# A two-layer hybrid decoder trunk in fp32 on one core: when the attention output of layer 0 is scaled by its norm and turned

## The chip, the cores and the metric

The kernel runs on one core of one Trainium2 chip. The metric is the device time of one execution in microseconds (us). Before the change the median of three runs is 2280.72 us (2280.49 to 2282.51).

## The reference, cut to what matters

The program runs a trunk of two layers over 1024 tokens of width 1024. Each layer norms its input, projects it, mixes it (layer 0: differential attention beside a causal pooling mixer), projects the mixer's output with `w_out`, adds it to the residual stream, and adds a SwiGLU FFN. The change lies between the attention of layer 0 and its output projection:

```python
# layer 0; 4 heads ("units"), values of width 128
def block(i):                                   # 128 queries
    s = einsum('bqmhd,bkmhd->bmhqk', qb, k) * scale - slopes * dist     # two maps m
    p = softmax(where(dist >= 0, s, -inf))
    a = p[:, 0] - lam * p[:, 1]
    return einsum('bhqk,bkhd->bqhd', a, v)
ya = diff_attention(q, k, v, lam, slopes)
ya = rmsnorm(ya, ev_subln_gain) * (1.0 - lambda_init)   # per head and token, over 128 values
yb = multiscale_pool(u, pool_w, pool_scale)
x = x + concatenate([ya, yb], -1) @ ev_w_out            # 1024 x 1024
x = x + swiglu_ffn(x, ...)
```

## The kernel before, in words

Every fp32 product is made of three products: each factor is split into a rounded high part and a low part (value minus high part), and high·high, high·low and low·high are summed (`mm3`). ScalarE (ACT) writes most high parts, VectorE (DVE) and GpSimd (POOL) the low parts. The five engines run programs of their own that are written out by hand in one fixed order each; semaphores with counts order them against each other. Nothing is scheduled by a planner.

**The attention of layer 0** runs over 32 tiles n = 8u + i: unit (head) u = 0 to 3, query block i = 0 to 7, with 128(i+1) keys. A tile passes through these steps: PE makes the scores of both maps (`score`, L971 and L972; two tiles ahead), DVE adds the bias and takes the maximum (`biased`, L2030), ACT takes the exponent (`expo`, L1505), DVE combines both maps (`combine`, L2052; counts `c_ok`), PE transposes the result into PSUM (`turn`, L991; waits for `c_ok`), ACT copies it to SBUF (`turned`, writes PT), PE multiplies it with the values (`weigh`, L1007), and ACT squares the result and writes it, divided by the softmax denominator, to Y (`scaled`: L1536, then the copy Y; counts `o_ok`). From tile 9 on, PE also computes one block of the output projection of the pooling half beside each tile (`out_block`, 12 products of 128x256, 32 blocks in all), which DVE adds to X (`add_block`, L2059). Blocks 0 to 22 run beside the attention, 23 to 31 behind it.

**Norm and turn of Y.** GpSimd makes 1/rms of a unit from its sums of squares (`unit_power(u)`, L859 and L861, counts `y_rs`). Behind the last tile and three `add_block`s DVE multiplies Y by it, one instruction for each of the 8 token blocks over all four units (L2163, counts `y_ok`). Then PE transposes Y, unit by unit (`turn_y(j)`, L1171, 8 transpositions, all four wait for the 8 instructions); ACT writes the high part HH of a turned unit with the sub-norm's gain (`y_hi`, copy HH), DVE the low part HL (`y_lo`, L2133). Two units fit in PSUM banks 0 to 3, which the scores use before, so `turn_y(2)` and `turn_y(3)` wait for `y_lo(0)` and `y_lo(1)`. The turns stand between the blocks 27, 28, 30 and 31.

**Output projection of the attention half.** For two token blocks PE first makes the products with the weight group `WOh`, `WOl` (units 0 and 1, `out_part(2, ...)`), then those with `WO3h`, `WO3l` (units 2 and 3, `out_part(3, ...)`), 24 products of 128x512 each; the next six token blocks take both together. It waits once, for all four `y_lo`. GpSimd writes the low parts of these groups: `WO3l` (`low_w("g3", ...)`) before `unit_power(3)`, `WOl` (`low_w("g2", ...)`) behind it, each as soon as ACT's high part is there. The norm of the FFN follows.

## Time and profile before

| | |
|---|---|
| runs (median; lowest to highest) | 2280.72 us; 2280.49 to 2282.51 |
| the profiled execution: its own time, and its span | 2289.15 us, 2287.4 us |
| granted TensorE clock, mean | 0.983 of full speed |
| busy: PE / DVE / ACT / POOL | 2204.0 / 1268.6 / 884.5 / 795.8 us |
| attention of layer 0, and the stretch behind it up to the FFN | from about 227 us to 440 us of the span |

The span goes from the first to the last instruction; 1.75 us of the execution's own time lie around it. PE (TensorE, products) is busy for 96% of the span; its loads of weights (PEld) lie beside. In the rows of a timeline the columns are the start in us of the span, the duration, the engine, the line, the operation, the output and its inputs, and how many such instructions follow in a row; a bracket gives the idle time of the engine just before and what ended it. The ends of PE instructions are modelled and overlap the next start, so for PE the distance from start to start is what counts.

### The profile page before, as it was taken

To read this page: it belongs to the slowest core of one execution; us is meant where nothing else is said; L and a number is where in the kernel's file an instruction comes from. 1 tells how busy PE (TensorE), PEld (TensorE's weight loads), DVE (VectorE), ACT (ScalarE), POOL (GpSimd) and SP (SyncE) were. 2 spreads that over 40 slices of the span, in tenths; PEclk is the share of its full clock that TensorE was granted. 3 is DMA by queue.
4 is the path that set the end of the run, shared out by engine and by line. 5 is a ranking of instruction groups with operands and counts; after the bars stand their busy time and mean duration, and the time that the engine had idled before them with its cause. 6 is when DMAs were issued, how large, how long until landed. Compare 5 with 4: busy or idle time off the path is not lost.

```text
span 2287.4 us, 30362 instructions
## 1 busy us (share of the span) xinstructions
PE 2204.0 (96%) x10600; PEld 1840.3 (80%) x10600; DVE 1268.6 (55%) x1771; ACT 884.5 (39%) x1443; POOL 795.8 (35%) x538
## 2 busy tenths in 40 slices
PE   7999897999999999999999998999999999999999
PEld 6876787888888887888888877887888888887887
DVE  4244775676656554558322336566775555554555
ACT  4123874443333333435211126662443333333433
POOL 0022542266666772002000131220367766762000
PEclk9999899999999999999999998999999999999999
DMA  5021120035555547674111111102045555547665
GB/s 178 10 78 28 38 84 19 19 121 192 194 193 167 165 159 272 192 239 137 37 44 48 46 55 38 38 19 74 19 147 194 193 196 164 166 154 267 193 192 194
DMA packets 219222, 283.87 MB, mean 124 GB/s; under 512 B 11504, under 2 KB 120560, under 8 KB 219120
## 3 DMA queue, kind: packets, MB, share of 16 engines
q1 hardware_dynamic: 218832, 282.50, 38.3%
q8 instruction: 58, 0.95, 0.2%
q14 instruction: 44, 0.36, 0.1%
q10 hardware_dynamic: 288, 0.05, 0.0%
HBM read 199.67 MB, written 73.40 MB: 119 GB/s over the span
## 4 chain that ended last, share of the span: by engine, by line
PE 71%; issue 21%; DVE 4%; ACT 2%; POOL 2%; DMA 0%; POOLq 0%; DVEq 0%; SPq 0%; ACTq 0%
PE PS L1284 12%; PE PS L1285 12%; PE PS L1286 12%; PE PS L1311 6%; PE PS L1313 6%; PE PS L1312 6%; PE PS L1007 3%; PE PS L919 3%; PE PS L921 3%; PE PS L920 3%; PE PS L991 2%; POOL QRS L832 1%; PE PS L971 1%; PE PS L972 1%; PE PS L937 1%
## 5 line engine op out<-in xcount | busy, mean ns | idle before, releaser
L1799 DVE TENSOR_TENSOR LINEl<-LINE,HIGH 128x1024 fp32r<-128x1024 f32 x154 | 193.8, 1264 | 170.2 <-ACT HIGH L1342 169.9
L1342 ACT ACTIVATE HIGH<-LINE 128x1024 fp32r<-128x1024 f32 x154 | 162.5, 1059 | 236.6 <-PE PS L1313 232.2
L1311 PE MATMUL PS<-HIGH 128*128 128x512 f32 x616 | 241.8, 393 | 7.0 <-DVE LINEl L1799 7.0
L1312 PE MATMUL PS<-LINEl,HIGH 128*128 128x512 f32 x616 | 240.8, 391 | 0.0
L1313 PE MATMUL PS<-HIGH,LINEl 128*128 128x512 f32 x616 | 240.8, 391 | 0.0
L1799 DVE TENSOR_TENSOR SLOTl<-BLOCKS,RING 128x512 fp32r<-128x512 f32 x168 | 157.7, 939 | 96.8 <-ACT RING L1342 92.0
L807 POOL TENSOR_TENSOR ST<-ST 128x512 f32<-128x512 f32 x132 | 191.9, 1454 | 34.4 <-DMA ST<-in_ffn_w_down 25.7
L1342 ACT ACTIVATE RING<-BLOCKS 128x512 fp32r<-128x512 f32 x168 | 105.9, 631 | 227.7 <-PE PS L1286 223.6
L832 POOL TENSOR_TENSOR QRS<-QMS,EXPO 128x8 f32<-128x8 f32 x32 | 52.0, 1639 | 383.3 <-DVE QMS L1962 383.2
L1799 DVE TENSOR_TENSOR SLOTl<-SLOT,RING 128x512 fp32r<-128x512 f32 x126 | 134.4, 1066 | 86.6 <-ACT RING L1342 86.3
L1311 PEld LDWEIGHTS PS<-HIGH 128*128 128x128 f32 x616 | 116.3, 189 | 32.0 <-DVE LINEl L1799 8.3
L1313 PEld LDWEIGHTS PS<-HIGH,LINEl 128*128 128x128 f32 x616 | 116.3, 189 | 24.6
L1312 PEld LDWEIGHTS PS<-LINEl,HIGH 128*128 128x128 f32 x616 | 116.5, 189 | 24.2
L1007 PE MATMUL PS<-V,PT 128*128 (+1 forms) x864 | 118.2, 284 | 13.4 <-ACT Y L1342 11.6
L1007 PEld LDWEIGHTS PS<-V,PT 128*128 128x128 f32 x864 | 111.0, 200 | 24.5 <-ACT PT L1342 14.1
L1284 PE MATMUL PS<-B1h,RING 128*128 128x512 f32 x336 | 130.7, 389 | 0.0
L1285 PE MATMUL PS<-B1l,RING 128*128 128x512 f32 x336 | 130.7, 389 | 0.0
L1286 PE MATMUL PS<-B1h,SLOTl 128*128 128x512 f32 x336 | 130.7, 389 | 0.0
L1342 ACT ACTIVATE RING<-SLOT 128x512 fp32r<-128x512 f32 x126 | 79.2, 630 | 125.3 <-PE PS L1286 114.9
L779 POOL TENSOR_TENSOR SLOT<-BLOCKS 128x512 f32<-128x512 f32 x42 | 55.2, 1314 | 190.3 <-DMA BLOCKS<-in_ffn_w_up 190.3
L2030 DVE CUSTOM_DVE_ANT_0 PR<-PS,BIAS 128x128 f32<-128x128 f32 (+7 forms) x130 | 96.9, 748 | 31.1 <-PE PS L991 16.5
L812 POOL TENSOR_TENSOR RST<-MSQ,EXPO 128x1 f32<-128x1 f32 x32 | 22.9, 718 | 260.9 <-DVE MSQ L1816 260.9
(299 smaller groups left out, 5711.7 us busy)
## 6 DMA issues: line engine op xcount, KB each, us to landing
LINE<-hidden SPq DMA_DIRECT2D x154, 256.0 KB, 2.7
hidden<-HID SPq DMA_DIRECT2D x44, 512.0 KB, 4.4
ST<-in_ffn_w_down SPq DMA_DIRECT2D x44, 512.0 KB, 4.2
sums<-ST SPq DMA_DIRECT2D x22, 1024.0 KB, 6.1
hidden<-ST SPq DMA_DIRECT2D x22, 1024.0 KB, 6.7
LINE<-sums SPq DMA_DIRECT2D x88, 256.0 KB, 3.0
BLOCKS<-in_ffn_w_gate SPq DMA_DIRECT2D x42, 512.0 KB, 4.0
BLOCKS<-in_ffn_w_up SPq DMA_DIRECT2D x42, 512.0 KB, 5.2
```

The source lines that it names most:

```text
L807: nc.gpsimd.tensor_tensor(dst, x, y, op).then_inc(st_sum, 1)
L832: nc.gpsimd.tensor_tensor(QRS[:, 8 * b:8 * b + 8], QMS[:, 8 * b:8 * b + 8], EXPO[:, 0:8], ALU.pow).then_inc(qk_rs, 1)
L1007: last = pe.matmul(weighed(L, m, i), PT[m if L else i % 2][:, P * j:P * j + P], V[:, j, bass.ds(off, w)], start=(j == 0), stop=(j == i))
L1284: pe.matmul(dst, lh, rh[:, k, :], start=k == 0 and not adds_on, stop=False, skip_group_check=adds_on)
L1285: pe.matmul(dst, lh, rl[:, k, :], start=False, stop=False, skip_group_check=adds_on)
L1286: last = pe.matmul(dst, ll, rh[:, k, :], start=False, stop=k == 3, skip_group_check=adds_on)
L1311: pe.matmul(dst, hi[:, 0, ts], hi[:, 1, :], start=j == 0 and not adds_on, stop=False, skip_group_check=adds_on)
L1312: pe.matmul(dst, hi[:, 0, ts], lo[:, 1, :], start=False, stop=False, skip_group_check=adds_on)
L1313: pe.matmul(dst, lo[:, 0, ts], hi[:, 1, :], start=False, stop=j == NJ - 1, skip_group_check=adds_on).then_inc(dn_pe, 1)
L1342: return nc.scalar.activation(dst, src, ACT.Copy, **kw)
L1799: return v.tensor_tensor(dst, src, hi.bitcast(F32), ALU.subtract)
L2030: v.tensor_tensor_reduce(out=PR[m][t % 2][:, 0:keys], in0=PS[:, 1024 * m:1024 * m + keys], in1=table, scale=-1.0, scalar=3.0e38, op0=ALU.a ...
```

## The change

It moves the scaling and the turning of Y forward, and holds two low parts on GpSimd back:

- DVE scales Y by unit instead of by token block: `unit_scaled(u)` is one multiplication of 128 x 8 x 128 values. Units 0, 1 and 2 are scaled inside the attention, behind `combine` of tiles 14, 22 and 29; unit 3 behind blocks 23 to 25. `y_ok` now counts units.
- PE turns unit 0 before `turn` of tile 31, unit 1 before the last `weigh`, unit 2 behind block 25 and unit 3 behind block 28. The first two wait until DVE has read the last scores.
- ACT writes the high parts of units 0 and 1 before and behind the copy and scaling of tile 30's values; DVE writes their low parts ahead of `add_block(23)`.
- The products with `WOh`, `WOl` wait for the low parts of units 0 and 1 only, those with `WO3h`, `WO3l` for all four.
- GpSimd waits for `combine` of tile 31 (`c_ok`, 32) before `WO3l`, and for all four scalings (`y_ok`, 4) before `WOl`.

```diff
 # GpSimd
                     low_w("q3", QWl[3], QWs[3], QWh[3])
+                    pool.wait_ge(c_ok, TILES0)
                     low_w("g3", WO3l, WO3s, WO3h)
                     unit_power(3)
+                    pool.wait_ge(y_ok, UNITS)
                     low_w("g2", WOl, WO2s, WOh)
 # TensorE
+                def turn_y(j):
+                    if L == 0:
+                        pe.wait_ge(y_ok, j + 1)
+                        if j < 2:
+                            for m in range(2):
+                                pe.wait_ge(s_mx[m][0], 1 + TILES0)
...
+                            if g + i == TILES0 - 1:
+                                turn_y(0)
                             turn(0, 0, g, 0, i)
                             if g + i >= FILL_FROM:
                                 out_block(g + i - FILL_FROM)
+                    turn_y(1)
                     weigh(0, 0, UNITS - 1, NT * (UNITS - 1), 0, NT - 1)
...
-                    for blocks in ((23, 24, 25, 26, 27), (28,), (29, 30), (31,)):
-                        for k in blocks:
-                            out_block(k)
-                        turn_y((27, 28, 30, 31).index(blocks[-1]))
+                    for k in range(BLOCKS_IN, 4 * NT):
+                        out_block(k)
+                        if k in (25, 28):
+                            turn_y((25, 28).index(k) + 2)
...
-                pe.wait_ge(yt_lo, 4 * L + 4)
+                pe.wait_ge(yt_lo, 4 * L + (2, 4)[L])
                 pe.wait_ge(wo_lo, WO_AT[L] + (6, 3)[L])
...
+                pe.wait_ge(yt_lo, 4 * L + 4)
                 pe.wait_ge(wo_lo, WO_AT[L] + (6, 4)[L])
 # ScalarE
+                    score_done()
+                    y_hi(0)
                     turned(0, NT * (UNITS - 1), NT - 1)
-                    for n in (TILES0 - 2, TILES0 - 1):
-                        scaled(n)
+                    scaled(TILES0 - 2)
+                    y_hi(1)
+                    scaled(TILES0 - 1)
                     high_w("g2", WOh, WO2s)
 # VectorE
+                def unit_scaled(u):
+                    dve.wait_ge(y_rs, u + 1)
+                    dve.wait_ge(o_ok[0][0], 2 + NT * (u + 1))
+                    ys = Y[:, :, P * u:P * u + P]
+                    by = YRS[:, NT * u:NT * u + NT].rearrange("p (t o) -> p t o", o=1).broadcast_to([P, NT, P])
+                    v.tensor_tensor(ys, ys, by, ALU.mult).then_inc(y_ok, 1)
...
                         combine(i)
+                        if n in (14, 22, 29):
+                            unit_scaled(u - 1)
...
+                    y_lo(0)
+                    y_lo(1)
                     for k in range(23, 26):
                         add_block(k)
-                    dve.wait_ge(y_rs, UNITS)
-                    dve.wait_ge(o_ok[0][0], 2 + 8 * UNITS)
-                    for t in range(NT):
-                        ys = Y[:, t, :].rearrange("p (h d) -> p h d", d=P)
-                        by = YRS[:].rearrange("p (h t) -> p h t", t=NT)[:, :, t:t + 1].broadcast_to([P, 4, P])
-                        v.tensor_tensor(ys, ys, by, ALU.mult).then_inc(y_ok, 1)
-                    for j, blocks in enumerate(((26, 27), (28,), (29, 30), (31,))):
-                        for k in blocks:
-                            add_block(k)
-                        y_lo(j)
+                    unit_scaled(UNITS - 1)
+                    y_lo(2)
+                    for k in range(26, 29):
+                        add_block(k)
+                    y_lo(3)
+                    for k in range(29, 32):
+                        add_block(k)
```

What it moves on each engine, as the built programs have it. PE at tile 31, before: the last products of tile 30 with the values (V, PT), the transposition of the combined map (PR), block 22 (QWh, QWl with UH, UL), the products of tile 31, block 23.

```order
L1007 MATMUL PS<-V,PT_286 128x128 [waits o_okA0,t_eaA0]
L1007 MATMUL PS<-V,PT_286 128x128 x6
L991 MATMUL PS<-IDN,PR_291 128x128 [waits c_ok,t_eaA0]
L991 MATMUL PS<-IDN,PR_291 128x128 x7
L919 MATMUL PS<-QWh_81,UH_63 128x256 [waits od_add0]
L920 MATMUL PS<-QWl_77,UH_63 128x256
...
L1007 MATMUL PS<-V,PT_287 128x128 [waits o_okA0,t_eaA0]
L1007 MATMUL PS<-V,PT_287 128x128 x7
L919 MATMUL PS<-QWh_81,UH_63 128x256 [waits od_add0]
```

PE at the same place now (Y is the scaled attention output, IDN the identity):

```order
L1010 MATMUL PS<-V,PT_286 128x128 [waits o_okA0,t_eaA0]
L1010 MATMUL PS<-V,PT_286 128x128 x6
L1129 MATMUL PS<-IDN,Y 128x128 [waits s_mxB0,s_mxA0,y_ok]
L1129 MATMUL PS<-IDN,Y 128x128 x7
L994 MATMUL PS<-IDN,PR_291 128x128 [waits c_ok,t_eaA0]
L994 MATMUL PS<-IDN,PR_291 128x128 x7
L922 MATMUL PS<-QWh_81,UH_63 128x256 [waits od_add0]
L923 MATMUL PS<-QWl_77,UH_63 128x256
...
L1129 MATMUL PS<-IDN,Y 128x128 [waits s_mxB0,s_mxA0,y_ok]
L1129 MATMUL PS<-IDN,Y 128x128 x7
L1010 MATMUL PS<-V,PT_287 128x128 [waits o_okA0,t_eaA0]
L1010 MATMUL PS<-V,PT_287 128x128 x7
```

Two groups of 8 transpositions of Y have come in, one in front of tile 31's transposition and one in front of its products with the values; they wait for `y_ok` and for the maxima of both maps (`s_mx`).

DVE from `combine` of tile 31 on, before (PR: the maps; X with PS: a block added; HL: a low part of turned Y):

```order
L2052 SCALAR_TENSOR_TENSOR PR_291<-PR_291,SCB,PR_289 128x1024 [waits att_seq0]
L2059 TENSOR_TENSOR X<-PS,X 128x256 [waits od_pe0]
L2059 TENSOR_TENSOR X<-PS,X 128x256 [waits od_pe0,att_seq0]
L2059 TENSOR_TENSOR X<-PS,X 128x256 [waits od_pe0] x2
L2163 TENSOR_TENSOR Y<-Y,YRS 128x512 [waits o_okA0,y_rs]
L2163 TENSOR_TENSOR Y<-Y,YRS 128x512 x7
L2059 TENSOR_TENSOR X<-PS,X 128x256 [waits od_pe0] x2
L2133 SCALAR_TENSOR_TENSOR HL<-PS,COLS,HH 128x1024 [waits yt_hi]
L2059 TENSOR_TENSOR X<-PS,X 128x256 [waits od_pe0]
L2133 SCALAR_TENSOR_TENSOR HL<-PS,COLS,HH 128x1024 [waits yt_hi]
```

and now:

```order
L2073 SCALAR_TENSOR_TENSOR PR_291<-PR_291,SCB,PR_289 128x1024 [waits att_seq0]
L2080 TENSOR_TENSOR X<-PS,X 128x256 [waits od_pe0]
L2092 SCALAR_TENSOR_TENSOR HL<-PS,COLS,HH 128x1024 [waits s_mxA0,s_mxB0,yt_hi,att_seq0]
L2092 SCALAR_TENSOR_TENSOR HL<-PS,COLS,HH 128x1024 [waits s_mxB0,s_mxA0,yt_hi]
L2080 TENSOR_TENSOR X<-PS,X 128x256 [waits od_pe0] x3
L2103 TENSOR_TENSOR Y<-Y,YRS 128x8x128 [waits o_okA0,y_rs]
L2092 SCALAR_TENSOR_TENSOR HL<-PS,COLS,HH 128x1024 [waits o_peA0,yt_hi]
L2080 TENSOR_TENSOR X<-PS,X 128x256 [waits od_pe0] x3
L2092 SCALAR_TENSOR_TENSOR HL<-PS,COLS,HH 128x1024 [waits o_peA0,yt_hi]
L2080 TENSOR_TENSOR X<-PS,X 128x256 [waits od_pe0] x3
```

The 8 multiplications of 128x512 are gone from here; one of 128x8x128 is left, and two low parts of Y stand ahead of blocks 23 to 25. Three more such multiplications stand further up, each behind a `combine`.

GpSimd from the low part of the pooling half's last weight group (QWl) on, before:

```order
L853 TENSOR_TENSOR QWl_78<-QWs_74,QWh_82 128x1024 [waits wo_hi,y_rs]
L853 TENSOR_TENSOR WO3l<-WO3s,WO3h 128x2048 [waits wo_hi,wo_lo]
L859 TENSOR_TENSOR YSS<-YSS,EPSP 128x8 [waits y_sq,wo_lo]
L861 TENSOR_TENSOR YRS<-YSS,EXPO 128x8 [waits y_ms]
L853 TENSOR_TENSOR WOl<-WO2s,WOh 128x2048 [waits wo_hi,y_rs]
```

and now:

```order
L853 TENSOR_TENSOR QWl_78<-QWs_74,QWh_82 128x1024 [waits wo_hi,y_rs]
L853 TENSOR_TENSOR WO3l<-WO3s,WO3h 128x2048 [waits wo_hi,c_ok,wo_lo]
L859 TENSOR_TENSOR YSS<-YSS,EPSP 128x8 [waits y_sq,wo_lo]
L861 TENSOR_TENSOR YRS<-YSS,EXPO 128x8 [waits y_ms]
L853 TENSOR_TENSOR WOl<-WO2s,WOh 128x2048 [waits wo_hi,y_ok,y_rs]
```

The rows are the same five; two of them have one more semaphore to wait for, `c_ok` and `y_ok`.

## Rows read from the trace of the kernel before

**Rows 1.** The page's chain that ended last, by engine.

```profile
PE 71%; issue 21%; DVE 4%; ACT 2%; POOL 2%; DMA 0%; POOLq 0%; DVEq 0%; SPq 0%; ACTq 0%
```

**Rows 2.** Timeline of PE, 361 to 410 us.

```profile
361.34 1.80 PE L1007 MATMUL PS<-V,PT 128*128 128x128 f32 x14 [1.55 <-ACT Y L1342]
365.66 1.06 PE L991 MATMUL PS<-IDN,PR 128*128 128x128 f32 x8 [2.52 <-DVE PR L2052]
366.48 0.36 PE L919 MATMUL PS<-QWh,UH 128*128 128x256 f32 x1
...
368.54 2.02 PE L1007 MATMUL PS<-V,PT 128*128 128x128 f32 x16 [0.38 <-ACT Y L1342]
370.32 0.36 PE L919 MATMUL PS<-QWh,UH 128*128 128x256 f32 x1
...
377.24 0.28 PE L919 MATMUL PS<-QWh,UH 128*128 128x256 f32 x1
...
382.69 1.97 PE L1171 MATMUL PS<-IDN,Y 128*128 128x128 f32 x8 [4.93 <-DVE Y L2163]
...
388.25 0.36 PE L919 MATMUL PS<-QWh,UH 128*128 128x256 f32 x1
...
391.20 1.04 PE L1171 MATMUL PS<-IDN,Y 128*128 128x128 f32 x8
391.99 0.36 PE L919 MATMUL PS<-QWh,UH 128*128 128x256 f32 x1
...
393.50 1.04 PE L1171 MATMUL PS<-IDN,Y 128*128 128x128 f32 x8
397.06 0.50 PE L919 MATMUL PS<-WOh,HH 128*128 128x512 f32 x1 [2.52 <-DVE HL L2133]
...
404.26 0.39 PE L919 MATMUL PS<-WO3h,HH 128*128 128x512 f32 x1
...
409.70 0.39 PE L919 MATMUL PS<-WOh,HH 128*128 128x512 f32 x1
```

**Rows 3.** Stretches: from:to, length, busy of each engine, granted clock, DMA.

```profile
356.00:370.00 14.00, 9.55 (x78) 8.92 (x79) 7.81 (x7) 6.83 (x13) 4.51 (x1) 1.00 0.00 1
382.00:388.00 6.00, 5.31 (x25) 5.31 (x26) 3.01 (x6) 1.11 (x1) 0.00 (x0) 0.51 0.01 3
398.30:401.50 3.20, 3.20 (x9) 2.42 (x9) 0.00 (x0) 0.00 (x0) 0.00 (x0) 0.50 0.00 0
```

**Rows 4.** Timeline of DVE, tiles 22, 23, 30 and 31, and the tail.

```profile
321.86 1.14 DVE L2052 SCALAR_TENSOR_TENSOR PR<-PR,SCB,PR 128x896 f32<-128x896 f32 x1
...
325.62 0.42 DVE L2059 TENSOR_TENSOR X<-PS,X 128x256 f32<-128x256 f32 x1 [0.80 <-PE PS L921]
...
354.45 1.23 DVE L2030 CUSTOM_DVE_ANT_0 PR<-PS,BIAS 128x1024 f32<-128x1024 f32 x1 [0.82 <-PE PS L991]
...
360.17 5.34 DVE L2052 SCALAR_TENSOR_TENSOR PR<-PR,SCB,PR 128x1024 f32<-128x1024 f32 x1
...
375.26 7.38 DVE L2163 TENSOR_TENSOR Y<-Y,YRS 128x512 f32<-128x512 f32 x8
...
395.73 1.28 DVE L2133 SCALAR_TENSOR_TENSOR HL<-PS,COLS,HH 128x1024 fp32r<-128x1024 f32 x1 [0.68 <-ACT HH L1342]
```

**Rows 5.** Timeline of GpSimd, 324 to 378 us.

```profile
324.59 4.59 POOL L839 TENSOR_TENSOR QST<-QK,QST 64x768 fp32r<-64x768 f32 x2 [2.76 <-issue]
...
359.93 4.51 POOL L853 TENSOR_TENSOR WO3l<-WO3s,WO3h 128x2048 fp32r<-128x2048 f32 x1 [8.65 <-ACT WO3h L1342]
...
373.27 4.61 POOL L853 TENSOR_TENSOR WOl<-WO2s,WOh 128x2048 fp32r<-128x2048 f32 x1
```

**Rows 6.** Timeline of ACT, 366 to 386 us.

```profile
366.76 1.02 ACT L1342 ACTIVATE PT<-PS 128x1024 f32<-128x1024 f32 x1 [5.57 <-PE PS L991]
...
368.03 0.37 ACT L1342 ACTIVATE Y<-PS,RDN 128x128 f32<-128x128 f32 x1
...
384.78 1.11 ACT L1342 ACTIVATE HH<-PS,COLS 128x1024 fp32r<-128x1024 f32 x1 [11.65 <-PE PS L1171]
```

More of the change, by code:

```diff
@@ L1111, in out_block @@
                     last.then_inc(od_pe[0], 1)
+                def turn_y(j):
[4 more added lines that the diff above has]
+                                pe.wait_ge(s_mx[m][0], 1 + TILES0)
+                    else:
+                        pe.wait_ge(o_ok[0][1], 2 + 8 * UNITS)
+                        pe.wait_ge(o_ok[1][1], 2 + 8 * UNITS)
+                    if j >= 2:
+                        pe.wait_ge(yt_lo, 4 * L + j - 1)
+                    for t in range(NT):
+                        last = pe.transpose(PS[:, 1024 * (j % 2) + P * t:1024 * (j % 2) + P * t + P], Y[:, t, P * j:P * j + P], IDN[:])
+                    last.then_inc(yt_pe, 1)
                 if L == 0:
@@ L1547, in high_w, with y_hi, score_done @@
                     copy(dst[:], src[:]).then_inc(wo_hi, 1)
+                def y_hi(j):
+                    act.wait_ge(yt_pe, 4 * L + j + 1)
+                    kw = dict(scale=SUBG[:, 0:1]) if L == 0 else {}
+                    copy(HH[:, (0, 4)[L] + j, :], PS[:, 1024 * (j % 2):1024 * (j % 2) + 1024], **kw).then_inc(yt_hi, 1)
+                def score_done():
+                    for m in range(2):
+                        act.wait_ge(s_pe[m][0], TILES0)
+                    act.wait_ge(staged[0], 128)
+                    act.wait_ge(stack_lo, STACK_AT[1])
                 if L == 0:
@@ L2059, in add_block, with y_lo @@
                     v.tensor_tensor(xs, block_out(n), xs, ALU.add).then_inc(od_add[0], 1)
+                def y_lo(j):
+                    dve.wait_ge(yt_hi, 4 * L + j + 1)
+                    src, c = PS[:, 1024 * (j % 2):1024 * (j % 2) + 1024], (0, 4)[L] + j
+                    if L == 0:
+                        if j < 2:
+                            for m in range(2):
+                                dve.wait_ge(s_mx[m][0], 1 + TILES0)
+                        else:
+                            dve.wait_ge(o_pe[0][0], TILES0 + j - 3)
+                        v.scalar_tensor_tensor(out=HL[:, c, :], in0=src, scalar=SUBG[:, 0:1], in1=HH[:, c, :].bitcast(F32),
+                                               op0=ALU.mult, op1=ALU.subtract).then_inc(yt_lo, 1)
+                    else:
+                        low(HL[:, c, :], src, HH[:, c, :]).then_inc(yt_lo, 1)
+                def unit_scaled(u):
[4 more added lines that the diff above has]
+                    v.tensor_tensor(ys, ys, by, ALU.mult).then_inc(y_ok, 1)
                 if L == 0:
```

27 lines of the change are left out of this document (2 added, 25 removed).

## The prediction

> **What bounds the kernel now.** I read the page's chain first: 71% of what ended last is PE and 21% is issue, most of it between PE instructions [rows 1]. So only what lets PE start its next product earlier counts. Then the stretches around the place of the change, then the timeline of PE there, and for each gap the engine named in its bracket.
>
> PE runs dense until the last two tiles of the attention. From there to the first product with WOh at 397.06 it has four gaps of interest [rows 2]. (a) It waits 1.55 us before the values of tile 30, for ACT. (b) It waits 2.52 us before the transposition of tile 31 at 365.66, for DVE's `combine`. (c) It waits 4.93 us before the first transposition of Y at 382.69, for the scaling. (d) It waits 2.52 us before 397.06, for the last low part. In 356 to 370 us PE is busy for only 9.55 of 14 us, yet its granted clock stays at 1.00, the 2.4 GHz level. Behind gap (c) it is 0.51, and 0.50 again behind gap (d), the 1.2 GHz level [rows 3].
>
> What makes (b) and (c) long stands on DVE and GpSimd. `combine` of tile 31 takes 5.34 us from 360.17; GpSimd writes WO3l from 359.93 to 364.44, and `combine` ends 1.07 us behind that. The eight scalings take 7.38 us from 375.26, while GpSimd writes WOl until 377.88 [rows 4, 5]. Both DVE operations have two inputs in SBUF and so have GpSimd's.
>
> **The change part by part.** Times are those of the profiled execution: span 2287.4 us, 2289.15 us with the 1.75 us around it, 8.4 us above the median of the runs. I take differences from it and subtract them from the median.
>
> 1. *Up to the values of tile 31.* The values of tile 31 (16 instructions) take 368.54 to 370.32, 1.78 us, so those of tile 30 (14), which still start at 361.34, leave PE free 1.56 us later, at 362.90 [rows 2]. There the new transposition of unit 0 stands: 391.20 to 391.99, 0.79 us, until 363.69. `combine` of tile 31 is free of GpSimd now. I take 1.3 us for it (896 columns took 1.14, and 1024 columns with one PSUM input 1.28 [rows 4]), so it is done at 361.5 and PE need not wait. The transposition of tile 31 takes 0.82 (365.66 to 366.48), until 364.51. Block 22 takes 1.46: from 370.32 to 377.24 lie 19 groups of three products at 0.364 us, four groups a block. Unit 1's transposition follows until 366.76. On ACT the high part of unit 0 starts when its transposition ends, 363.94 (the row's 1.04), and takes 1.11; the copy PT of tile 31 starts at 365.05; before, the values of tile 31 started 1.78 us behind the start of that copy (366.76 to 368.54) [rows 2, 6]. That gives 366.83, just behind PE's own 366.76. Gain 368.54 - 366.83 = 1.71 us, with two groups of transpositions of Y already done.
> 2. *Gap (c).* The last group before it starts at 377.24 and needs 0.36, so PE stands from 377.60 to 382.69: 5.09 us gone.
> 3. *Gap (d).* From 393.50 + 0.79 = 394.29 to 397.06: 2.77 us gone.
> 4. *Two groups of transpositions* that stood behind the values of tile 31 stand before them: 2 x 0.79 = 1.58 us.
> 5. *Clock behind (c).* From 382.69 to 388.25, 5.56 us, PE did two groups of transpositions and one block. At the full clock these take 0.79 + 1.51 (391.99 to 393.50) + 0.79 = 3.09. Gain 2.47 us.
> 6. *Clock behind (d).* The 24 products with WOh took 7.20 us (397.06 to 404.26), the next 24 took 5.44 (to 409.70). Gain 1.76 us [rows 2].
>
> Sum 1.71 + 5.09 + 2.77 + 1.58 + 2.47 + 1.76 = 15.4 us.
>
> *What the gain uncovers.* After: values of tile 31 366.83 to 368.61, three blocks (4.4) to 373.0, unit 2 turned to 373.8, three blocks to 378.2, unit 3 turned to 379.0, three blocks to 383.4, then WOh. Is anything late? Before, WOl started 4.73 us behind the values of tile 31 (368.54 to 373.27) directly behind `unit_power(3)` [rows 2, 5]; so the norm of unit 3 is there at 371.6. DVE scales unit 3 behind block 25 (done 373.0, add 0.42, scaling 1.3): 374.7. PE wants it at 378.2: 3.5 us to spare. GpSimd's WOl then takes 4.61, until 379.3, wanted at 383.4: 4.1 to spare. Its neighbours on DVE read PSUM and one SBUF input; such adds took 0.42 as ever [rows 4]. The low part of unit 3: 379.0 + 1.11 + 1.28 = 381.4, wanted 5.44 us behind 383.4: 7 to spare. What follows the first 48 products keeps its distances to them, and PE is dense there.
>
> *The three scalings inside the attention* are not in the trace in this form (8 x 128 values, with strides). Bounds: 1.14 us, the 896-column `combine`, and 5.34, the blocked one. I take 1.3, near the first, since no GpSimd row lies beside these places. Behind tile 22 `combine` ends at 323.00, the scaling at 324.3; DVE idles 0.80 us before the add at 325.62 alone. Behind tile 29 DVE idles 0.82 us before the maximum at 354.45 [rows 4]; 0.5 us is left, and PE's own backlog covers most of it. On the path I take 0, at most 0.5 each (1.5), and no gain below 0 is seen there: nothing goes away in these tiles. The added waits on PE and ACT are for counts long reached; GpSimd's wait for `c_ok` puts WO3l at 361.5 to 366.0, before the values of tile 31 are done, with nothing else queued behind it that is wanted earlier.
>
> **The rivals.**
>
> *R1, the clock does not stay up.* The idle times of 356 to 366 us remain in part (1.55 us before tile 30's values), and the work there gets denser but not dense. For it: the clock fell behind (c) and (d), the latter only 2.52 us long. Against: 1.00 all through 356 to 370 us, with gaps of 1.55 and 2.52 us [rows 3]. If 3 to 6 us of full-speed work run at half level somewhere, the gain is 9.4 to 12.4: about 2270.
>
> *R2, scaling and low part meet.* Behind tile 22 the scaling would end about 0.3 us before GpSimd's pair of stack low parts starts at 324.59 (2 in 4.59 us) [rows 5]; tile 14 is built alike. If GpSimd came first, DVE would wait for one of them, 2.3 us, and be late by 2.3 + 1.3 - 0.8 = 2.8 us; twice is 5.6: 2270.9. Against: the scaling has nothing to wait for and starts well ahead.
> The Trainium skill has a rule for this, and the blocked `combine` and scaling of the rows agree with it: in "SBUF — State Buffer", section "Who interferes with whom", a VectorE instruction with two SBUF inputs and a GpSimd one that reads SBUF exclude each other for the whole instruction, and the one that starts first wins. By that rule the scaling, if first, would delay GpSimd instead, which speaks for my 0 at these tiles, and for 5.6 if the order turned.
>
> *R3, the change does not do what it says:* `combine` of tile 31 is slow for another reason and stays at 5.34. Then tile 31 is transposed at 365.66 as before, unit 1 until 366.48 + 1.46 + 0.79 = 368.73, and item 1 gives -0.2 instead of 1.7: 2267.2. Against: its end 1.07 us behind GpSimd's.
>
> *R4, a new wait in the tail:* unit 3's chain is later than worked out by 6 us or so and PE waits 2 to 3 us: 2268.
>
> *R5, slower.* Place: PE from 366.8 on. If its clock fell to the half level in the sparse stretch before and stayed there through the blocks and the first 24 products, 16.6 + 5.4 = 22 us of full-speed work would take 44: 2280.7 - 15.4 + 22 = 2287. It decides against the change from 15.4 us of work at half level on. Against: the low stretches lasted about 6 and 3.2 us, and the work from 366.8 on has no gap.
> The Trainium skill, "TensorE: Matmul & The Clock Gate", section "What's actually happening", says that the low clock is the default and activity releases it; by that rule the thinned stretch before 366 us could start it. No row of this stretch shows it.
>
> **How the numbers follow.** Forecast 2280.7 - 15.4 = 2265.3: 0.63. R1 0.15, R2 0.07, R3 0.05, R4 0.05, R5 0.03, and 0.02 that all is spent again within 0.2%. This kernel's runs can tell about 0.2%, 4.6 us, from no change: the bound is 2276.2. Faster 0.94, same 0.02, slower 0.04 (R5, and a share of what I don't see). Range: the runs before spread by 2 us; upward 1.5 for the scalings, then R3, R4 and most of R1 and R2: 2272. Downward, terms 2 to 6 are read off and can only grow if other waits shorten: 2261.
>
> **What would show it.** Right: `combine` of tile 31 near 1.3 us; values of tile 31 some 1.7 us earlier relative to those of tile 30; no idle of PE over 0.5 us from there to the first product with WOh, 16.6 us later, and a granted clock of 1.00 throughout; each scaling near 1.3 us; first WO3h product 27.5 us behind the start of tile 30's values instead of 42.9. Wrong: a 0.5 clock there (R1, R5), a scaling over 2 us (R2), a bracket naming Y, HL or WOl before a PE row (R4), or waits of PE within tiles 14 to 16 or 22 to 24 that the trace before does not have.

## The result, and the profile after

The changed kernel takes 2268.90 us (median of 5 runs, 2267.12 to 2271.86); the kernel before took 2282.51 us on the same chip (5 runs, 2280.49 to 2285.86). The ratio is 0.9942, 95% interval 0.9931 to 0.9954: 13.2 us less (0.0058 x 2282.51), between 10.5 and 15.7. Forecast were 15.4 us less and 2265.3 us, range 2261 to 2272.

The profiled execution has an own time of 2268.90 us, a span of 2267.1 us and a mean clock of 0.988. Its span is 20.3 us shorter than that of the execution read before (2287.4). The rows below say which part of that is the change.

The page: the totals of the engines (busy us, share of the span, instructions).

```profile
PE 2192.8 (97%) x10600; PEld 1831.4 (81%) x10600; DVE 1261.3 (56%) x1767; ACT 883.8 (39%) x1443; POOL 794.5 (35%) x538
```

PE is busy for 11.2 us less than before (2204.0) although it does the same products: some of the work that ran at the low clock, here and in layer 1, runs at the high one in this execution. The chain of waits is PE 71% and issue 21%, as in [rows 1]. Now the place itself. Stretches of the kernel after (from:to, length, busy of PE, PEld, DVE, ACT, POOL with counts, granted clock, DMA share, GB/s):

```profile
356.00:370.00 14.00, 12.46 (x109) 12.16 (x108) 5.84 (x8) 9.93 (x19) 5.24 (x3) 1.00 0.00 1
361.00:405.00 44.00, 44.00 (x291) 40.33 (x292) 19.39 (x29) 15.73 (x23) 13.19 (x7) 1.00 0.09 25
```

The same stretch of the kernel before:

```profile
361.00:405.00 44.00, 33.30 (x218) 30.98 (x219) 20.82 (x23) 8.82 (x13) 9.89 (x4) 0.88 0.09 25
```

In the same 44 us the trace has 291 PE instructions instead of 218, PE has no idle time, and its clock is 1.00 instead of 0.88. Timeline of PE after, answering to [rows 2]:

```profile
360.96 1.80 PE L1010 MATMUL PS<-V,PT 128*128 128x128 f32 x14 [1.54 <-ACT Y L1353]
362.59 1.04 PE L1129 MATMUL PS<-IDN,Y 128*128 128x128 f32 x8
363.46 1.04 PE L994 MATMUL PS<-IDN,PR 128*128 128x128 f32 x8
...
365.77 1.04 PE L1129 MATMUL PS<-IDN,Y 128*128 128x128 f32 x8
366.65 1.95 PE L1010 MATMUL PS<-V,PT 128*128 128x128 f32 x16
...
372.74 1.03 PE L1129 MATMUL PS<-IDN,Y 128*128 128x128 f32 x8
...
377.92 1.03 PE L1129 MATMUL PS<-IDN,Y 128*128 128x128 f32 x8
...
383.10 0.40 PE L922 MATMUL PS<-WOh,HH 128*128 128x512 f32 x1
...
388.57 0.39 PE L922 MATMUL PS<-WO3h,HH 128*128 128x512 f32 x1
```

Gap (a), 1.54 us for ACT, is still there. The brackets of (b), (c) and (d) are gone. The distance that the prediction named, from the values of tile 30 to the first product with WO3h, is 388.57 - 360.96 = 27.61 us (forecast 27.5, before 42.92). I call it D below. It is free of what the clock does elsewhere in a run, so it serves as the measure of the experiments; the ratio of whole runs is the second, coarser one.

Timeline of DVE after, answering to [rows 4]: the scalings behind tiles 22 and 29, `combine` of tile 31, and the scaling of unit 3.

```profile
321.49 1.14 DVE L2073 SCALAR_TENSOR_TENSOR PR<-PR,SCB,PR 128x896 f32<-128x896 f32 x1
322.55 1.22 DVE L2103 TENSOR_TENSOR Y<-Y,YRS 128x1024 f32<-128x1024 f32 x1
...
325.26 0.42 DVE L2080 TENSOR_TENSOR X<-PS,X 128x256 f32<-128x256 f32 x1 [0.81 <-PE PS L924]
...
351.62 1.21 DVE L2103 TENSOR_TENSOR Y<-Y,YRS 128x1024 f32<-128x1024 f32 x1
...
359.79 1.28 DVE L2073 SCALAR_TENSOR_TENSOR PR<-PR,SCB,PR 128x1024 f32<-128x1024 f32 x1
...
373.28 1.22 DVE L2103 TENSOR_TENSOR Y<-Y,YRS 128x1024 f32<-128x1024 f32 x1
```

Each scaling takes 1.21 or 1.22 us, `combine` of tile 31 1.28 instead of 5.34. DVE still waits 0.81 us for PE before the add behind tile 22, as it did before (0.80): the scaling costs nothing there. Timeline of GpSimd after, answering to [rows 5]:

```profile
361.20 4.55 POOL L853 TENSOR_TENSOR WO3l<-WO3s,WO3h 128x2048 fp32r<-128x2048 f32 x1 [10.32 <-DVE PR L2073]
...
374.63 4.61 POOL L853 TENSOR_TENSOR WOl<-WO2s,WOh 128x2048 fp32r<-128x2048 f32 x1 [3.48 <-DVE Y L2103]
```

Both low parts now wait for DVE, as their brackets say. WO3l ends at 365.75 and meets no DVE operation at all: DVE is idle from the end of `combine` at 361.07 to the add at 365.98. WOl (374.63 to 379.24) runs beside DVE operations that read PSUM, a low part HL at 375.05 with 1.28 us and adds with 0.42, both as before.

**Where the other 4.7 us of the span come from.** D accounts for 15.3 of the 20.3 us. From 0 to 361 us both traces agree within 0.4 us, and the start of the FFN keeps a lead of 15.6. The rest arises in the attention of layer 1. The stretch 1320 to 1560 us, first of the kernel before, then of the kernel after (the same in time, so it begins some 15 us later in the work of the kernel after):

```profile
1320.00:1560.00 240.00, 217.79 (x1359) 189.96 (x1360) 132.04 (x353) 129.63 (x260) 53.44 (x33) 0.91 0.15 40
```

```profile
1320.00:1560.00 240.00, 217.19 (x1391) 189.62 (x1390) 144.50 (x367) 129.80 (x257) 52.26 (x32) 0.94 0.14 36
```

The clock is 0.91 against 0.94. The change touches nothing there; the next section shows that it is not the change's doing.

### The profile page after: what moved, and what is told of

Its sections match the earlier page's. It is cut to its first block, busy times and chain, and to the rows that moved or that the text cites. A ratio compares the mean times of both kernels' runs of the same rounds, so it can differ in the third digit from the quotient of the medians.

```text
span 2267.1 us, 30371 instructions
## 1 busy us (share of the span) xinstructions
PE 2192.8 (97%) x10600; PEld 1831.4 (81%) x10600; DVE 1261.3 (56%) x1767; ACT 883.8 (39%) x1443; POOL 794.5 (35%) x538
## 4 chain that ended last, share of the span: by engine, by line
PE 71%; issue 21%; DVE 3%; ACT 2%; POOL 2%; DMA 0%; POOLq 0%; DVEq 0%; SPq 0%; ACTq 0%
PE PS L1295 12%; PE PS L1297 12%; PE PS L1296 12%; PE PS L1322 6%; PE PS L1324 6%; PE PS L1323 6%; PE PS L1010 3%; PE PS L922 3%; PE PS L924 3%; PE PS L923 3%; PE PS L994 2%; POOL QRS L832 1%; PE PS L974 1%; PE PS L975 1%; PE PS L940 1%
## 5 line engine op out<-in xcount | busy, mean ns | idle before, releaser
L1820 DVE TENSOR_TENSOR SLOTl<-SLOT,RING 128x512 fp32r<-128x512 f32 x126 | 140.4, 1114 | 85.9 <-ACT RING L1353 85.6
```

The source lines that it names most:

```text
L1820: return v.tensor_tensor(dst, src, hi.bitcast(F32), ALU.subtract)
```

## The experiments

My theory was that of the prediction: two exclusions between DVE and GpSimd, one wait for the scaling, one wait for the last low part, and the clock behind these two waits. The rivals: the waits on GpSimd do nothing (R3), scalings inside the attention cost time (R2), the clock matters more or less than read, and the gain of layer 1 belongs to the change. Every kernel below was run 5 to 9 times beside the kernel before; the ratio is its time over that of the kernel before on the same chip, with its 95% interval.

### The changed kernel once more

No edit: the changed kernel on the chip of the next three.

> The changed kernel once more, as the control of this study. D is the distance from the first product of tile 30's values to the first product with WO3h: 42.92 us before, 27.61 us in the first profile after. My theory: D again 27.6, all clock 1.00 in between, and any difference of the whole time from 15.3 us comes from the half-clock stretches of layer 1's attention, whose place and length differ from execution to execution (44.4 us of half clock before, 30.7 after, between the start and the end of that stage). Rival: layer 1 is faster because of the change; then its half-clock time is again about 31 us here, and about 44 in kernels without the change.

Measured: 2269.11 us, ratio 0.9940 (0.9927 to 0.9954), D 390.69 - 363.08 = 27.61 us. The profiled execution was a longer one (own time 2274.7, span 2272.9 us). Its stretch in layer 1:

```profile
1320.00:1560.00 240.00, 219.93 (x1388) 192.28 (x1388) 139.82 (x362) 129.67 (x258) 52.31 (x32) 0.91 0.14 36
```

The same program at 0.91, like the kernel before. D is the same to 0.01 us. So D belongs to the program, at least where the clock inside it is 1.00, and the clock in layer 1 to the execution; the rival that the change speeds layer 1 up falls. Two of the kernels below have before's code in layer 1, the one with the two waits alone and the one with its gaps filled, and their profiled executions had 0.95 there.

### The two waits alone

The kernel before, with GpSimd's two waits:

```diff
                     low_w("q3", QWl[3], QWs[3], QWh[3])
+                    pool.wait_ge(c_ok, TILES0)
                     low_w("g3", WO3l, WO3s, WO3h)
                     unit_power(3)
+                    pool.wait_ge(y_ok, NT)
                     low_w("g2", WOl, WO2s, WOh)
```

> The kernel before with nothing but GpSimd's two waits: WO3l waits for combine of tile 31, WOl for the eight scalings. Theory (GpSimd blocks the DVE operations with two SBUF inputs): combine takes 1.3 instead of 5.3 us, tile 31's values start 2.8 us earlier, the scalings take 4.9 instead of 7.4 us, the first product with WOh comes 7.8 us earlier, and the clock behind the shorter gaps may stay up: D from 42.9 to 33.4 to 35.2. Rival (combine and the first scaling are slow for a reason of their own, say their access patterns): they stay at 5.3 and 3.2 us and D at 42.9.

Measured: 2275.34 us, ratio 0.9974 (0.9962 to 0.9985), D 396.41 - 359.55 = 36.86 us. Its timelines, DVE first, then PE:

```profile
358.38 1.28 DVE L2054 SCALAR_TENSOR_TENSOR PR<-PR,SCB,PR 128x1024 f32<-128x1024 f32 x1
...
370.74 4.89 DVE L2165 TENSOR_TENSOR Y<-Y,YRS 128x512 f32<-128x512 f32 x8
```

```profile
375.69 1.74 PE L1173 MATMUL PS<-IDN,Y 128*128 128x128 f32 x8 [2.45 <-DVE Y L2165]
...
389.23 0.50 PE L921 MATMUL PS<-WOh,HH 128*128 128x512 f32 x1 [2.52 <-DVE HL L2135]
```

The waits do what they say: `combine` 5.34 to 1.28 us, the eight scalings 7.38 to 4.89. Gap (c) is halved, to 2.45 us. But D missed the upper end of its expectation by 1.7 us, since I had let the clock stay up behind the shorter gap. It did not. A stretch of this kernel right behind gap (c), and one right behind gap (d):

```profile
375.69:379.50 3.81, 3.81 (x20) 3.81 (x20) 1.42 (x3) 1.11 (x1) 3.73 (x1) 0.55 0.02 4
389.20:392.70 3.50, 3.47 (x9) 2.75 (x10) 0.00 (x0) 0.00 (x0) 0.00 (x0) 0.56 0.00 0
```

Gaps of 2.45 and 2.52 us were enough, each behind dense work. Before the change the gap of 2.52 us ahead of tile 31, in thin work, had left the clock at 1.00 [rows 2, 3]. The length of a gap alone doesn't tell. Nor does the density of the work ahead of it: in the kernel before, the values of tile 6 stand behind a gap of 2.47 us, also in thin work, and there the clock fell. The row, then 7 us of work ahead of this gap and the stretch behind it, then 7 us ahead of the gap before tile 31:

```profile
255.58 3.32 PE L1007 MATMUL PS<-V,PT 128*128 128x128 f32 x14 [2.47 <-ACT Y L1342]
```

```profile
246.10:253.10 7.00, 5.68 (x42) 4.72 (x40) 5.88 (x12) 6.81 (x15) 2.99 (x3) 1.00 0.01 2
255.58:261.50 5.92, 5.92 (x26) 5.59 (x26) 1.11 (x5) 1.99 (x6) 4.34 (x2) 0.50 0.00 0
356.10:363.10 7.00, 5.45 (x45) 5.00 (x44) 4.87 (x6) 5.10 (x9) 3.17 (x1) 1.00 0.01 2
```

PE was busy for 5.68 and 5.45 of 7 us, and the clock behind the gap was 0.50 in one place and 1.00 in the other. What decides between them stays open.

How long the low clock lasts differs between executions, too. Behind the same gap at tile 6 it is 0.50 over 255.20 to 261.20 us of the changed kernel, and 0.72 in the mean of 254.00 to 260.00 of the kernel "changed, one wait" below, whose program is the same up to there; the values of tiles 6 and 7 are 7.27 and 6.34 us apart. So D is sure to 0.01 us only where the clock in it stays at 1.00. In the kernel before, in this one and in that with the turns in the tail and one wait, a low stretch lies inside D, and each of them was profiled once: their D, and with them terms 5 and 6, could differ by a microsecond or two in another execution (an estimate: behind gap (c) the low clock cost 2.47 us in the kernel before).

### All but the two waits

The changed kernel without them:

```diff
-                    pool.wait_ge(c_ok, TILES0)
                     low_w("g3", WO3l, WO3s, WO3h)
                     unit_power(3)
-                    pool.wait_ge(y_ok, UNITS)
                     low_w("g2", WOl, WO2s, WOh)
```

> The changed kernel without GpSimd's two waits. Theory: combine of tile 31 takes 5.3 us again and holds tile 31's transposition; tile 31's values start 1.7 to 1.9 us later; unit 3's scaling meets WOl and waits for it (3 to 4 us instead of 1.2) but is wanted only later. D 29.4, with a half-clock stretch up to 31. Rival (the waits are worth nothing): D 27.6. Rival (unit 3's blocked scaling is on the path too): D 31 to 33 with an idle before the last transpositions of Y.

Measured: 2271.72 us, ratio 0.9949 (0.9936 to 0.9963), D 387.06 - 357.59 = 29.47 us. DVE, PE and GpSimd:

```profile
356.43 5.34 DVE L2071 SCALAR_TENSOR_TENSOR PR<-PR,SCB,PR 128x1024 f32<-128x1024 f32 x1
...
371.76 3.69 DVE L2101 TENSOR_TENSOR Y<-Y,YRS 128x1024 f32<-128x1024 f32 x1
```

```profile
361.91 1.06 PE L992 MATMUL PS<-IDN,PR 128*128 128x128 f32 x8 [1.65 <-DVE PR L2071]
```

```profile
356.17 4.51 POOL L853 TENSOR_TENSOR WO3l<-WO3s,WO3h 128x2048 fp32r<-128x2048 f32 x1 [8.66 <-ACT WO3h L1351]
...
369.76 4.61 POOL L853 TENSOR_TENSOR WOl<-WO2s,WOh 128x2048 fp32r<-128x2048 f32 x1
```

GpSimd's low parts end at 360.68 and 374.37, the DVE operations 1.09 and 1.08 us behind them, at 361.77 and 375.45. So R3 (that `combine` is slow for a reason of its own) falls in both directions: with the wait it is short, without it long, in either program. On top of the moves the waits are worth only 29.47 - 27.61 = 1.86 us: the late scaling of unit 3 has room, only the late `combine` shows. Alone they were worth 6.06.

### The kernel before with its gaps filled

What the clock alone costs: before's program, its two gaps filled with transpositions of the identity whose result nobody reads.

```diff
+                def fill(col, n):
+                    for k in range(n):
+                        pe.transpose(PS[:, col + P * (k % 4):col + P * (k % 4) + P], IDN[:], IDN[:])
                 def turn_y(j):
                     if L == 0:
+                        if j == 0:
+                            fill(1024, 44)
                         pe.wait_ge(y_ok, NT)
...
+                if L == 0:
+                    pe.wait_ge(yt_lo, 3)
+                    fill(0, 16)
                 pe.wait_ge(yt_lo, 4 * L + 4)
```

> The kernel before with PE kept at work in both gaps: 44 transpositions of the identity into a free bank ahead of the first transposition of Y, 16 ahead of the first product with WOh; no wait changes, nothing reads them. Theory (the idle PE is what lets the clock fall, and this cost 2.5 + 1.8 us): clock 1.00 from 360 to 410 us, D 38.7. Rival (the clock falls on its own schedule or for the thin stretch before 366 us): half-clock stretches stay and D is 42.9.

Measured: 2277.55 us, ratio 0.9979 (0.9968 to 0.9989), D 400.34 - 361.44 = 38.90 us. PE, and the whole stretch:

```profile
377.69 4.96 PE L1164 MATMUL PS<-IDN 128*128 128x128 f32 x44
...
382.78 1.09 PE L1177 MATMUL PS<-IDN,Y 128*128 128x128 f32 x8
...
394.76 0.50 PE L919 MATMUL PS<-WOh,HH 128*128 128x512 f32 x1 [0.34 <-DVE HL L2142]
```

```profile
361.00:400.50 39.50, 35.46 (x275) 33.49 (x276) 20.82 (x23) 8.91 (x14) 9.98 (x4) 1.00 0.10 28
```

The first real transposition stands 14.14 us behind tile 31's values, as before (14.15), but the clock is 1.00 throughout and D is 4.02 us shorter. Terms 5 and 6 of the prediction had 4.23. Adding work that computes nothing made the program faster, by the price of the low clock. The rival (the clock falls on its own schedule, or for the thin stretch before 366 us) falls for these two places.

### Turns back in the tail, with the wait split and not split

The changed kernel with `turn_y(0)` to `turn_y(3)`, `y_hi` and `y_lo` back behind blocks 27, 28, 30 and 31, as before; the early scalings and GpSimd's waits stay. First with the split wait for the low parts:

```diff
-                            if g + i == TILES0 - 1:
-                                turn_y(0)
...
-                    turn_y(1)
...
-                        if k in (25, 28):
-                            turn_y((25, 28).index(k) + 2)
+                        if k in (27, 28, 30, 31):
+                            turn_y((27, 28, 30, 31).index(k))
```

> The changed kernel with the four turns of Y behind blocks 27, 28, 30 and 31 as before; the scalings by unit inside the attention, GpSimd's waits and the split wait for the low parts stay. Theory: PE is dense in either order, so moving the turns forward is worth only what they fill of PE's waits at tile 31, 0.3 to 0.4 us: D 28.0 (27.61 with the change). Rival (the turns must be early, or the low parts come too late for the tail): D 30 or more, with an idle before WO3h or WOh.

Measured: 2269.02 us, ratio 0.9942 (0.9929 to 0.9956), D 389.14 - 360.92 = 28.22 us, 0.2 above the expectation; PE has no gap before WOh or WO3h, so the rival falls.

Then with one wait for all four, as before:

```diff
-                pe.wait_ge(yt_lo, 4 * L + (2, 4)[L])
+                pe.wait_ge(yt_lo, 4 * L + 4)
```

> The kernel of e5, and PE waits for all four low parts ahead of the products with WOh, as the kernel before. Theory: the last low part comes 2.8 us behind the last turn and this gap opens again, with the half clock behind it as in the kernel before: D 28.0 + 2.8 + 1.7 = 32.5 (30.8 if the clock stays up). Rival (the split wait is worth nothing): D as in e5.

Measured: 2272.69 us, ratio 0.9955 (0.9942 to 0.9969), D 391.58 - 359.20 = 32.38 us. PE, and the stretch behind the gap:

```profile
384.64 0.79 PE L922 MATMUL PS<-WOh,HH 128*128 128x512 f32 x1 [2.53 <-DVE HL L2087]
```

```profile
384.60:388.10 3.50, 3.46 (x9) 2.81 (x10) 0.00 (x0) 0.00 (x0) 0.00 (x0) 0.57 0.00 0
```

Gap (d) and the clock behind it come back as the unsplit wait does: 4.16 us.

### One wait for the four low parts in the changed kernel

The same one-line edit, with the turns where the change put them.

> The changed kernel, but PE waits for all four low parts ahead of the products with WOh. Theory: with unit 3 turned behind block 28 its low part ends at 381.4, 1.7 us before PE comes to WOh, so this wait costs nothing: D 27.6. So early turns and split wait close the same gap, either would do. Rival (the split wait is needed in the changed kernel too): D 29 or more.

Measured: 2267.96 us, ratio 0.9934 (0.9921 to 0.9948), D 386.50 - 358.88 = 27.62 us. The split wait is worth nothing once the turns are early, and 4.16 us when they are not. Either edit alone removes gap (d): early turns save 4.76 us with one wait (32.38 - 27.62) and 0.61 with the split one (28.22 - 27.61).

### The scalings beside GpSimd's low parts

This is R2 forced to happen: units 0 and 1 are scaled one tile later.

```diff
-                        if n in (14, 22, 29):
+                        if n in (15, 23, 29):
```

> The changed kernel with the scalings of units 0 and 1 one tile later: behind the combine of tiles 15 and 23 instead of 14 and 22 (unit 2 stays at tile 29). In the trace of the changed kernel GpSimd's pair of stack low parts runs there (289.63 and 324.21 us, 4.59 us for two) and the combine of tiles 15 and 23 lies in it with 1.48 and 1.53 us, against 1.28 for that of tile 31 alone. Theory (the two engines exclude each other for one instruction at a time when both have two inputs in SBUF): the scaling, queued behind that combine, meets the second low part and takes 2 to 3 us instead of 1.22, or the low part does; DVE's idle time before the next adds (0.8 and 0.7 us) and PE's backlog hide most of it: at most 1 us at each place, the start of tile 30's values to the first WO3h product stays at 27.6 us, and the whole is 2269 to 2271. Rival R2 as the prediction priced it: each meeting costs the path up to 2.8 us, whole 2274.5, and PE shows a new wait for DVE in tiles 15 to 17 and 23 to 25. Second rival: the low part is not disturbing at all (scaling stays 1.22, whole unchanged).

Measured: 2267.82 us, ratio 0.9939 (0.9926 to 0.9952), D 386.84 - 359.22 = 27.62 us. DVE and GpSimd at tile 23:

```profile
323.84 1.54 DVE L2073 SCALAR_TENSOR_TENSOR PR<-PR,SCB,PR 128x1024 f32<-128x1024 f32 x1
325.30 2.84 DVE L2103 TENSOR_TENSOR Y<-Y,YRS 128x1024 f32<-128x1024 f32 x1
...
329.42 0.42 DVE L2080 TENSOR_TENSOR X<-PS,X 128x256 f32<-128x256 f32 x1 [0.34 <-PE PS L924]
```

```profile
322.47 4.58 POOL L839 TENSOR_TENSOR QST<-QK,QST 64x768 fp32r<-64x768 f32 x2 [2.76 <-issue]
```

The scaling takes 2.84 us at tile 23 and 2.83 at tile 15 instead of 1.22, ending 1.09 and 1.07 us behind GpSimd's pair: it waited for the second low part. DVE's wait for PE before the next add shrinks from 0.67 to 0.34 us and nothing else happens. From the values of tile 8 to those of tile 30 the program takes 359.22 - 264.23 = 94.99 us, the changed kernel 360.96 - 266.01 = 94.95. So not even the 1 us that I had allowed is lost, and the whole is below the 2269 to 2271 us expected. R2's meeting is real, and its price of 2.8 us a tile was not: it is 0.

### The weight copy behind the scaling

Gap (a) is left. Its bracket names Y, the scaling of tile 29's values by the softmax denominator, which ACT does behind the copy PT. Ahead of both, ACT writes WO3h in 1.91 us:

```profile
357.49 1.91 ACT L1353 ACTIVATE WO3h<-WO3s 128x2048 fp32r<-128x2048 f32 x1
359.30 0.91 ACT L1353 ACTIVATE PT<-PS 128x896 f32<-128x896 f32 x1
```

(of the changed kernel). The edit moves that copy behind PT and the scaling of tile 29's values:

```diff
                             scaled(n - 2)
+                        if n == TILES0 - 1:
+                            for m in range(2):
+                                act.wait_ge(s_pe[m][0], TILES0)
+                            high_w("g3", WO3h, WO3s)
...
-                        elif n == 30:
-                            for m in range(2):
-                                act.wait_ge(s_pe[m][0], TILES0)
-                            high_w("g3", WO3h, WO3s)
```

> The changed kernel with ACT's copy WO3h (1.9 us) issued behind the scaling of tile 29's values instead of ahead of the copy PT of tile 30. T is the distance from the first transposition of tile 30's map to the first product with WO3h: 46.85 us before, 31.54 after. Theory: the 1.54 us that PE still waits before tile 30's values comes from this copy standing in ACT's order; ACT has 2.9 us of idle time a little later. T 30.4, about 1.1 us less. Rival (tile 30's values wait for something else, or the copy is only late elsewhere, at the high part of unit 0): T 31.5 or more. The whole time can tell 1.1 us from nothing only barely.

Measured: 2264.70 us (2263.96 to 2266.91), ratio 0.9920 (0.9907 to 0.9934). ACT and PE:

```profile
355.30 0.92 ACT L1353 ACTIVATE PT<-PS 128x896 f32<-128x896 f32 x1 [0.42 <-PE PS L994]
...
356.71 1.92 ACT L1353 ACTIVATE WO3h<-WO3s 128x2048 fp32r<-128x2048 f32 x1
```

```profile
354.31 0.95 PE L994 MATMUL PS<-IDN,PR 128*128 128x128 f32 x7
...
356.97 1.80 PE L1010 MATMUL PS<-V,PT 128*128 128x128 f32 x14 [0.28 <-ACT Y L1353]
```

PE waits 0.28 us instead of 1.54. D starts behind this gap and stays 27.61; counted from the transposition of tile 30 the way to WO3h is 384.58 - 354.31 = 30.27 us, against 388.57 - 357.03 = 31.54 in the changed kernel. That 1.27 us is what the trace gives to the edit, as expected. The whole runs show more: the kernel with one wait, whose D is the changed kernel's, had 2267.96 us on the same chip, 3.3 more. The intervals of the two ratios overlap (0.9907 to 0.9934 and 0.9921 to 0.9948), so the trace's number is the surer one. Of the kernels run this has the lowest median; its interval overlaps that of the changed kernel as well (0.9931 to 0.9954).

### The stack copies split as well

The same idea at the unit changes: in the trace of the changed kernel PE waits 1.32 us before the values of tiles 14 and 22, while ACT makes two stack copies ahead of PT. On top of the previous kernel the last one moves behind PT:

```diff
+                        if i == NT - 1 and u + 1 < UNITS:
+                            next_stack(g, (u + 1) % 2, u + 1, 5)
...
-                            next_stack(g, (u + 1) % 2, u + 1, *{1: (0,), 2: (1,), 3: (2, 3), 6: (4, 5)}.get(i, ()))
+                            next_stack(g, (u + 1) % 2, u + 1, *{1: (0,), 2: (1,), 3: (2, 3), 6: (4,)}.get(i, ()))
```

> The kernel with ACT's WO3h copy behind the scaling of tile 29's values, and in addition the last of the six stack copies of each next unit (QST, 0.85 us) moved behind the copy PT of tiles 6, 14 and 22 and the scaling that follows it. In the trace of the changed kernel PE waits 1.32 us before the values of tiles 14 and 22 (292.25 and 326.77) because ACT does two stack copies (1.70 us for both, from 323.24) before it copies PT (324.97). Theory (the same as for the WO3h copy: PE's wait ends with PT, so what stands ahead of PT on ACT counts one to one): each of the waits becomes 0.85 shorter, 1.7 to 2.5 us over two or three unit changes, whole 2262.5 against about 2264.7. Rival: GpSimd's last low part of the unit then starts up to 1.3 us later and PE gets a new wait of the same size before the scores of tiles 10, 18 and 26: whole unchanged. Second rival: nothing changes at tile 22, because the map transposition that feeds PT ends too late: waits stay at 1.32.

Measured: 2265.87 us (2261.35 to 2268.97), ratio 0.9923 (0.9911 to 0.9936), against 0.9920 (0.9907 to 0.9934) of the previous kernel. The whole runs show no gain, but with intervals of about 3 us to each side they can't tell the expected 1.7 to 2.5 us from nothing. The traces can tell more. From the values of tile 10 to the first product with WO3h, both at a clock of 1.00, the previous kernel takes 384.58 - 270.81 = 113.77 us and this one 385.27 - 272.77 = 112.50, 1.27 less. The waits at tiles 14 and 22 did shrink as expected, from 1.32 to 0.17 us, 1.15 each. A part was given back as the rival had it, though not by the rival's way. It stands at tile 17, on PE and on DVE, with GpSimd's row beside them:

```profile
301.31 0.41 PE L994 MATMUL PS<-IDN,PR 128*128 128x128 f32 x2 [1.23 <-DVE PR L2075]
```

```profile
299.30 1.86 DVE L2075 SCALAR_TENSOR_TENSOR PR<-PR,SCB,PR 128x256 f32<-128x256 f32 x1
```

```profile
298.50 2.38 POOL L853 TENSOR_TENSOR QWl<-QWs,QWh 128x1024 fp32r<-128x1024 f32 x1 [5.08 <-ACT QWh L1353]
```

DVE's `combine` of tile 17 started 1.88 us behind GpSimd's low part of a weight group in the previous kernel (298.50, 296.62) and starts 0.80 us behind it here, so that it meets more of it: it takes 1.86 us where it took 0.80 there and an undisturbed one of this width 0.47 (tile 25 of the changed kernel), and PE waits 1.23 us for it. Tiles 16 and 17 are 4.39 us apart instead of 3.35, so the exclusion takes 1.0 of the 2.3 us won at tiles 14 and 22.

Tile 9 shows the same meeting: `combine` takes 1.75 us instead of 1.12, and PE waits 1.03 us for it instead of 0.24. Tiles 8 to 9 take 5.80 us instead of 3.50, but only 0.8 of these 2.3 us are the wait. The rest is the clock, 0.50 from 265.60 to 269.00 us here and 1.00 beside the same products of the previous kernel (264.40 to 266.70). There the low clock had come earlier, behind the wait of 2.46 us at tile 6, which is 1.47 here. From the values of tile 5 to those of tile 10 this kernel takes 22.21 us and the previous one 22.94.

So in the traces this kernel is 2.0 us shorter from the values of tile 5 to WO3h (134.71 against 136.71 us), of which 1.27 don't hang on the clock. Its profiled execution is 1.9 us longer all the same (2266.10 against 2264.25 us). Part of that is clock ahead of the place of the edit, where both programs are the same: 0.98 over the first 200 us and 0.87 from 200 to 240, against 1.00 and 1.00. Whether the edit is worth its 1 to 2 us in the whole time is not shown.

## Why the prediction was right

D and its parts, all of profiled executions:

| kernel | D, us | less than before | ratio of before (95%) |
|---|---|---|---|
| before | 42.92 | | |
| changed, two executions | 27.61, 27.61 | 15.31 | 0.9942 (0.9931 to 0.9954), 0.9940 (0.9927 to 0.9954) |
| two waits alone | 36.86 | 6.06 | 0.9974 (0.9962 to 0.9985) |
| all but the two waits | 29.47 | 13.45 | 0.9949 (0.9936 to 0.9963) |
| before, gaps filled | 38.90 | 4.02 | 0.9979 (0.9968 to 0.9989) |
| turns in the tail, split wait | 28.22 | 14.70 | 0.9942 (0.9929 to 0.9956) |
| turns in the tail, one wait | 32.38 | 10.54 | 0.9955 (0.9942 to 0.9969) |
| changed, one wait | 27.62 | 15.30 | 0.9934 (0.9921 to 0.9948) |
| scalings at 15, 23 | 27.62 | 15.30 | 0.9939 (0.9926 to 0.9952) |

In every line the saving of D, divided by the 2283 us of the kernel before, lies inside the interval of the ratio. Point by point:

- *Term 1, up to the values of tile 31:* 1.71 forecast. They start 5.69 us behind those of tile 30 (366.65 - 360.96), before 7.20: 1.51. The step was right in what no longer holds PE, `combine`, and the gain was 0.2 us smaller: a group of eight transpositions takes 0.87 us here (362.59 to 363.46) and not 0.79, the values of tile 30 take 1.63 and not 1.56. The forecast had ACT's chain end last, 0.07 us behind PE; it was PE that came last, for the row at 366.65 has no bracket.
- *Terms 2 to 5, from there to the first product with WOh:* 5.09 + 2.77 + 1.58 + 2.47 = 11.91 forecast; 28.52 us became 16.45: 12.07. The 16.6 us of the forecast held.
- *Term 6:* 1.76 forecast; the 24 products took 5.47 us instead of 7.20: 1.73. The kernel with filled gaps shows terms 5 and 6 by themselves: 2.39 and 1.62 us (3.17 us from the first transposition of Y to block 29 instead of 5.56, and 5.58 for the 24 products instead of 7.20). Both are read from one execution of the kernel before; a low stretch of another length there would have moved them.
- *Sum:* 15.4 forecast, 15.31 measured in the trace, 13.2 (10.5 to 15.7) over whole runs. That the whole runs lie some 2 us below the trace, in both measurements of this kernel, is within their intervals, and I leave it open. The base matters too: the forecast starts from 2280.72 us, the median of three runs; with two more it is 2282.51, and that is 1.8 of the 3.6 us by which the time itself missed.
- *The exclusion of DVE and GpSimd:* shown both ways, by taking it out of before (5.34 to 1.28) and putting it back into after (1.28 to 5.34, 1.22 to 3.69). The rule of the Trainium skill that the prediction cited ("SBUF — State Buffer", section "Who interferes with whom") is borne out by these rows and by the scaling of 2.84 us that waited at tile 23.
- *The three scalings:* 1.3 us each taken, 1.21 to 1.22 found, and 0 on the path. The bound of 0.5 us each was not needed.
- *R1 and R5, the clock:* it is 1.00 from 356 us to 405 us. The thin stretch ahead of 366 us did not bring it down, with PE busy 12.46 us of 14. In the tail every gap of 2.45 us or more did: in the kernel before (c and d), in the one with the waits alone (c and d) and in the one with the turns in the tail and one wait (d), with 0.50 to 0.57 in the stretch behind it. In the changed kernel there is no such gap in the tail. Thin work was not safe in itself: the gap of 2.47 us at tile 6 lowered the clock, the one of 2.52 ahead of tile 31 did not, and the prediction leaned on the second alone. So R5's way, a low clock that stays, was not seen; R1's was right about the danger and wrong about the place.
- *R2:* the meeting happens if the scaling is moved by one tile, and costs nothing. The step of R2 that failed is its price: it took DVE's lateness for PE's, and PE has a backlog there.
- *R3, R4:* fall; the rows of `combine` and the absence of any bracket from 362 to 389 us say so.

The prediction says that PE runs dense until the last two tiles. It does not quite: waits of 2.47 us at tile 6 and of 1.33 at tiles 14 and 22 stand in the trace of the kernel before. The sum doesn't use this.

One thing the prediction does not say is which edit buys which gap. The edits overlap. The waits are worth 6.06 us alone and 1.86 beside the rest, 4.2 less; split wait and early turns each remove the same gap. The sum was right since it was taken over the gaps of the path, not over the edits.

## What to carry to other kernels

Add up the gaps of the bounding engine, not the merits of the edits; where two edits remove one gap, one of them is spare, and only a run without each tells which. A two-input DVE operation that meets a long two-input GpSimd one in SBUF inherits its end, so a wait that makes GpSimd come second is worth placing wherever the bounding engine waits for DVE; where it has a backlog the meeting is free. And any edit that shifts DVE against GpSimd by a microsecond can make such a meeting elsewhere: after the gain, look for the instruction that has grown.
